# Two passes over the weights become three, in a single-core decoder step (SSD scan, gMLP gating, expert retrieval)

## The chip, the cores and the metric

The kernel runs on one NeuronCore of a Trainium2 chip. The metric is the device time of one execution in microseconds, lower is better; the state before is given as the median of three executions. All data are float32.

## The reference, cut to what matters

One decoder layer is applied to 512 prompt tokens (one sequence) and to 8 samples of one token each, with the same weights (D = 2048).

```python
proj = x @ w_in                                   # z, xbc, dt, u, v, gates
xbc  = silu(causal_conv(xbc))                     # 4 taps
y, new_ssm = ssd_scan(xh, dt, A, B, C, state)     # chunks of 128 tokens, state carried on
y_a  = rms_per_group(y_with_skip * silu(z)) * w   # 8 groups
v    = layer_norm(gelu(v));  y_b = gelu(u) * (tril(W_s) @ v + b)     # per chunk of 128
mix  = (sigmoid(ga) * (y_a @ w_a) + sigmoid(gb) * (y_b @ w_b)) @ w_out
h    = layer_norm(alpha * x + mix)
# PEER: 8 heads pick 16 of 16384 experts each, by product keys
q = h @ w_q;  expert, gate = product_key_top16(q)
out  = sum_k gate_k * gelu(h . peer_u[expert_k]) * peer_v[expert_k]
y    = layer_norm(alpha * h + out)
```

Outputs are y of both groups, the last conv rows, the final SSD states of prompt and samples, and the normalised v of the last chunk. Every token gathers 128 rows of `peer_u` and 128 rows of `peer_v` of 8 KB each.

## The kernel before, in words

**Tiles.** All weights are laid out as 224 tiles of 128 output channels by 2048 inputs (1 MB). `gemm` (line 400, its matmul on L409) multiplies one tile by the activations of a pass: 16 matmuls of 128 x 128 weights with n columns, n being the tokens of the pass; a float32 matmul shows as two MATMUL instructions, each with a LDWEIGHTS, so a tile has 32 of each. The tiles come through a ring of three buffers (`load_weight`, L396) from SP's queue; tile p is loaded once tile p - 3 has been used.

**Passes.** Activations of all tokens don't fit into SBUF beside the rest, so the layer runs in two passes, each over all 224 tiles: pass A with 256 prompt tokens and the 8 samples (264 columns), pass B with the other 256 tokens. A pass has three stages, with a barrier after each: `ssd` (80 tiles), `sgu` (32 tiles) and `back` (112 tiles: 32 gates, 16 of w_b, 32 of w_a, 16 of w_out, 16 of w_q).

**Scan stage.** For each of 8 groups, TensorE projects B, C, four x tiles and four z tiles; ScalarE copies each to `raw` and makes the first tap, VectorE adds three (L1019), ScalarE applies silu (L927). Then for each chunk of 128 tokens `chunk_a` transposes and forms C B (L842 to L844), ScalarE makes the decays, VectorE weighs them (`weigh`, L1054 to L1056), and `chunk_b` multiplies (L857, L859, L860). The gated result is normalised (`rms` L865, `finish`) and stored to DRAM. A chunk's decay rows come by a DMA of 0.5 MB.

**The samples' scan** (pass A only) is GpSimd's: per group eight units of 4 samples x 128 states (128 x 512 elements): load the state, multiply by the decay (L1193), form x dt B (L1195), add (L1197), store (L1198), multiply by C (L1201); VectorE sums (L1037). B and C rows of a group go through DRAM (L1183, L1185), so that all partitions get them. The samples' eight columns are part of `xg` and `yg` and are normalised with the prompt's.

**SGU and back.** `sgu` projects V, normalises it (`ln_*`), projects U, mixes per chunk. `back` projects the gates, multiplies with both branches, adds and normalises to h, and in its last 16 tiles scores q against the keys and selects experts on VectorE (`Selection`, top 16 of each side, then of the 256 sums). The samples' selection is finished in pass B (`smp`).

**Experts.** There is one slot for each of the 512 tokens' j-th expert rows in a block (4 blocks x 128) and 8 slots for the samples: 520 in all. A slot gathers one `peer_u` row and one `peer_v` row for each of 128 tokens (two indirect DMAs of 1 MB, L250, from GpSimd's queue), and VectorE multiplies and sums with h (L306, 2.3 us) and adds the weighted v rows (L327, 2.35 us). Experts of a block can be fetched once that block's choice is done. So pass A has no slots; `plan` writes 260 slots by hand into the order of pass B (14 in each of the 8 scan groups, 20 + 20 in `sgu`, 32, 16, 32 and 16 with the tiles of `back`, 3 in the norm, 9 in the choice), and `tail` does the other 260 after the passes, with eight buffers each for u and v where the passes have four.

Of the kernel before, what the change touches and what calls it, by code (L numbers as in the profile page):

```python
# [25 lines left out]
P = 128  # L26
# [45 lines left out]
RING = 3  # L72
PASSES = 2
CP = CH // PASSES
NP = CP * P
# [8 lines left out]
SLOTS = CP * P  # L84
LAG = 6

# [14 lines left out]
class Pass:  # L101


    def __init__(self, i):
        self.i, self.smp = i, i == 0
        self.n = NP + (NS if self.smp else 0)
        self.first = NP * i
        self.col = 0 if i == 0 else NP + NS
        self.pos = N_TILES * i
        self.grp = N_GROUPS * i  # L110
        self.rows = [P] * CP + ([NS] if self.smp else [])
        self.nb = len(self.rows)

# [93 lines left out]

class Experts:
# [44 lines left out]
    def u_row(self, pool, s):  # L253

        if s < self.total:
            b, j = self.items[s]
            if not self.is_sample(s) and j % TOPK == 0:
                pool.wait_ge(self.k.head_done, PH * (b // CP) + j // TOPK + 1)
# [11 lines left out]
    def rows(self, pool, s, ahead, u_from=0):  # L270


        if s + ahead >= u_from:
            self.u_row(pool, s + ahead)
        if s - self.lag + ahead >= u_from:
            self.v_row(pool, s - self.lag + ahead)
# [71 lines left out]
class Kernel:  # L348
# [41 lines left out]
    def load_weight(self, sp, p):  # L390

        if p >= PASSES * N_TILES:
            return
        if p >= RING:
            sp.wait_ge(self.w_used, p - RING + 1)
        sp.dma_start(self.w_ring[:, p % RING, :],  # L396
                     self.a["w_tiles"][ORDER[p % N_TILES]]).then_inc(self.w_in[p % RING], 16)

    def gemm(self, pe, p, grp, x, n, start=True, stop=True, x_ready=None):
# [5 lines left out]
        pe.wait_ge(self.w_in[p % RING], 16 * (p // RING + 1))  # L405
        for k in range(KB):
            if x_ready:
                pe.wait_ge(*x_ready(k))
            last = pe.matmul(o, self.w_ring[:, p % RING, k * P:(k + 1) * P], x[:, k, :],  # L409
# [12 lines left out]
    def plan(self):  # L422
# [4 lines left out]
        def put(key, n):  # L427
            nonlocal s
            at[key] = range(s, s + int(n))
            s = at[key].stop  # L430

        for g in range(G):
            for c in range(9):
                put(("ssd", g, c), 1 + (c in (1, 3, 5, 7, 8)))
        for n in range(FT):
            put(("v", n), 1 + (n % 4 == 1))
        for n in range(FT):
            put(("u", n), 1 + (n % 4 == 1))
        for c in range(2 * FT):
            put(("gate", c), 1)  # L440
        for n in range(FT):
            put(("wb", n), 1)
        for n in range(FT):
            put(("wa", n), 2)
        for n in range(FT):
            put(("out", n), 1)
        put(("ln", 0), 2)
        put(("ln", 1), 1)
        for n in range(FT):
            put(("q", n), n >= 7)  # L450
# [3 lines left out]
    def steps(self, ps, *key):  # L454

        return self.at[key] if ps.i == 1 else ()

    def span(self, *names):

        every = [s for key, r in self.at.items() if key[0] in names for s in r]  # L460
        return range(min(every), max(every) + 1)


    def build(self):
# [12 lines left out]
        passes = [Pass(i) for i in range(PASSES)]  # L477
        self.pass_a = passes[0]
        with self.root:
# [20 lines left out]
            with ExitStack() as gemm:  # L500
                gs = lambda name, shape: gemm.enter_context(nc.sbuf_tensor(name, shape, F32))
                self.w_ring = gs("w_ring", [P, RING, WCOLS])
# [5 lines left out]
                with ExitStack() as st:  # L508
                    n = passes[0].n
                    cut = self.region(flat(rows_a))  # L510
                    xs, yb, m_acts = cut(KB, n), cut(KB, n), cut(KB * n)
                    spare = st.enter_context(nc.sbuf_tensor("spare", [P, KB * n], F32))[:]
                    self.tables(xs)
                    self.clear_sems()
                    self.one_pass(passes[0], xs, spare, yb, m_acts, None)
# [1397 lines left out]
```

## Time and profile before

| | us |
|---|---|
| median of 3 executions | 5422.86 (5422.43 to 5433.51) |
| profiled execution | 5416.87 |
| its span, first to last instruction | 5414.9 |
| TensorE busy | 3608.6 (67%) |
| VectorE busy | 3422.2 (63%) |
| GpSimd busy | 2398.3 (44%) |
| ScalarE busy | 702.4 (13%) |
| moved by DMA | 1672.07 MB, 309 GB/s on average |

Pass A lies between 56 and 1910 us of the span, pass B between 1910 and 4067, the tail after that. The busy shares are averages over these three parts, which have different limits; they must be read stage by stage. Matmuls are pipelined and their ends are modelled, so the distance between the starts of two groups of instructions tells more of TensorE's pace than the mean duration of one.

### The profile page before, as it was taken

The numbers are of one execution on the slowest core, as the hardware profiler recorded it, in microseconds if no ns is written. First come the engines' busy times: TensorE is split into PE (matmuls) and PEld (weight loads), VectorE is DVE, ScalarE is ACT, GpSimd is POOL, SyncE is SP. The second block draws the span as 40 slices with busy tenths as digits, with TensorE's granted clock in tenths as the row PEclk, the third lists the DMA queues.
The fourth block names the chain that finished last, engine by engine and source line by source line (L and its number), as shares of the span: only waits on it lengthen the run. The fifth ranks groups of instructions, "written<-read, shape, count | busy, mean of one in ns | idle before, by whom it ended". The sixth has DMA issues, their size and how long they took to land. (4 is left out here: it accounts for less than half of the span.)

```text
span 5414.9 us, 43573 instructions
## 1 busy us (share of the span) xinstructions
PE 3608.6 (67%) x16560; PEld 3028.1 (56%) x16560; DVE 3422.2 (63%) x4133; ACT 702.4 (13%) x1501; POOL 2398.3 (44%) x1504
## 2 busy tenths in 40 slices
PE   7999979999999968888778697897940000230000
PEld 5787768888887757667667586786740000000000
DVE  3455531000001859989867665565798999789999
ACT  2232321000000123333311010000100000000000
POOL 3575730000000025545543432443318888778885
PEclk8999989999999989999889898998975555565555
DMA  5565643344444379999989899999749999999998
GB/s 175 192 217 196 210 156 132 133 148 164 164 156 140 126 301 405 421 420 410 421 356 377 351 421 384 389 421 412 307 155 398 420 422 422 422 380 422 422 422 363
DMA packets 275097, 1672.07 MB, mean 309 GB/s; under 512 B 37041, under 2 KB 66225, under 8 KB 81969
## 3 DMA queue, kind: packets, MB, share of 16 engines
q0 software_dynamic: 161920, 1133.78, 51.2%
q1 hardware_dynamic: 112968, 535.51, 26.4%
q8 instruction: 131, 2.15, 0.2%
q14 instruction: 78, 0.63, 0.0%
HBM read 1633.31 MB, written 35.79 MB: 308 GB/s over the span
## 5 line engine op out<-in xcount | busy, mean ns | idle before, releaser
L250 POOL DMA_INDIRECT rows_a<-in_peer_u,expert x384 | 819.0, 2133 | 2182.4 <-POOLq L369 1149.2
L409 PE MATMUL psum<-rows_a,w_ring 128*128 128x264 f32 x7168 | 1625.5, 388 | 24.1 <-PEq L369 18.9
L409 PEld LDWEIGHTS psum<-rows_a,w_ring 128*128 128x128 f32 x7168 | 1367.2, 191 | 265.5 <-issue 30.5
L409 PE MATMUL psum<-x_acts,w_ring 128*128 128x256 f32 x5632 | 1257.4, 384 | 131.0 <-PEq L369 57.5
L409 PEld LDWEIGHTS psum<-x_acts,w_ring 128*128 128x128 f32 x5632 | 1084.0, 193 | 287.9 <-issue 83.4
L306 DVE SCALAR_TENSOR_TENSOR rows_a<-rows_a,h_tokens 128x2048 f32<-128x2048 f32 x384 | 878.7, 2289 | 106.1 <-DMA rows_a<-in_peer_u,expert 75.9
L250 POOL DMA_INDIRECT rows_a<-in_peer_v,expert x384 | 593.3, 1545 | 333.2 <-DVE h_tokens L327 165.1
L327 DVE SCALAR_TENSOR_TENSOR h_tokens<-rows_a,coef,h_tokens 128x2048 f32<-128x2048 f32 x256 | 602.6, 2354 | 79.4 <-issue 73.5
L1744 PE MATMUL psum<-acc,selector 8*128 8x512 f32 x64 | 57.5, 1075 | 683.8 <-DVE rows_a L306 479.0
L1744 PEld LDWEIGHTS psum<-acc,selector 8*128 8x128 f32 x64 | 19.9, 325 | 720.0 <-DVE rows_a L306 485.3
L1019 DVE SCALAR_TENSOR_TENSOR conv_acc<-raw,g_par,conv_acc 128x256 f32<-128x256 f32 x288 | 175.5, 609 | 283.8 <-ACT conv_acc L913 277.0
L327 DVE SCALAR_TENSOR_TENSOR acc<-rows_a,coef,acc 128x2048 f32<-128x2048 f32 x128 | 300.9, 2350 | 32.8 <-issue 30.2
L327 DVE SCALAR_TENSOR_TENSOR h_tokens<-rows_b,coef,h_tokens 128x2048 f32<-128x2048 f32 x128 | 300.9, 2351 | 20.2 <-issue 16.2
L306 DVE SCALAR_TENSOR_TENSOR rows_b<-rows_b,h_tokens 128x2048 f32<-128x2048 f32 x128 | 293.0, 2290 | 27.3 <-DMA rows_b<-in_peer_u,expert 22.6
L286 ACT ACTIVATE gelu<-dots 128x4 f32<-128x4 f32 x130 | 26.7, 205 | 2140.3 <-DVE rows_a L306 1517.1
L250 POOL DMA_INDIRECT rows_b<-in_peer_u,expert x128 | 265.5, 2074 | 81.5 <-issue 37.2
L250 POOL DMA_INDIRECT rows_b<-in_peer_v,expert x128 | 252.9, 1976 | 51.1 <-issue 37.4
L409 PE MATMUL psum<-branch_b,w_ring 128*128 128x256 f32 x1024 | 229.7, 385 | 43.6 <-DMA w_ring<-in_w_tiles 29.1
L409 PEld LDWEIGHTS psum<-branch_b,w_ring 128*128 128x128 f32 x1024 | 197.8, 194 | 72.6 <-issue 43.1
L1622 DVE TENSOR_TENSOR rows_a<-rows_a,psum 128x264 f32<-128x264 f32 x16 | 6.9, 429 | 338.3 <-PE psum L409 338.3
L1631 DVE TENSOR_TENSOR branch_part<-spare,psum 128x264 f32<-128x264 f32 x16 | 6.9, 429 | 214.2 <-PE psum L409 214.2
L409 PE MATMUL psum<-merged,w_ring 128*128 128x256 f32 x512 | 115.2, 384 | 1.8 <-DVE merged L1634 1.8
(368 smaller groups left out, 3024.8 us busy)
## 6 DMA issues: line engine op xcount, KB each, us to landing
w_ring<-in_w_tiles SPq DMA_DIRECT2D x448, 1024.0 KB, 6.3
smp_state<-in_state_ssm POOLq DMA_DIRECT2D x64, 256.0 KB, 5.7
out_ssm_sample<-smp_state POOLq DMA_DIRECT2D x64, 256.0 KB, 3.1
rows_a<-acum_rows_dram SPq DMA_DIRECT2D x16, 512.0 KB, 7.4
BC_bcast<-smp_bc_dram POOLq DMA_DIRECT2D x8, 1024.0 KB, 5.0
branch_b<-acum_rows_dram SPq DMA_DIRECT2D x16, 512.0 KB, 12.4
rows_a<-in_peer_u,expert POOLq DMA_INDIRECT x384, 20.6
rows_a<-in_peer_v,expert POOLq DMA_INDIRECT x384, 21.1
```

Of the source, the lines that this page charges most:

```text
L250: return pool.indirect_dma_start(out=dst, out_offset=None, in_=table, in_offset=bass.IndirectOffsetOnAxis(ap=self.index(s), axis=0))
L286: act.activation(self.ge[:, c], self.dots[:, c], ACT.Gelu).then_inc(self.gelu_done, 1)
L306: dve.scalar_tensor_tensor(out=u, in0=u, scalar=1.0, in1=h, op0=ALU.mult, op1=ALU.mult, accum_out=self.dots[:, s % 8:s % 8 + 1]).then_inc( ...
L327: dve.scalar_tensor_tensor(out=acc, in0=self.vrow[self.slot[s]], scalar=self.coef[:, s % 8:s % 8 + 1], in1=acc, op0=ALU.mult, op1=ALU.add) ...
L409: last = pe.matmul(o, self.w_ring[:, p % RING, k * P:(k + 1) * P], x[:, k, :], start=start and k == 0, stop=stop and k == KB - 1)
L1019: ins = dve.scalar_tensor_tensor(out=ac, in0=r[:, k:k + NP], scalar=w[:, k:k + 1], in1=ac, op0=ALU.mult, op1=ALU.add)
L1622: self.out_of_bank(dve.tensor_tensor(merged[:, m, :], merged[:, m, :], self.bank[(G_WB + m) % 2][:, 0:n], ALU.mult), G_WB + m)
L1631: self.out_of_bank(dve.tensor_tensor(part[:, m % 2, :], ga[:, m, :], self.bank[(G_WA + m) % 2][:, 0:n], ALU.mult), G_WA + m)
L1744: last = pe.matmul(self.bank[c], sel[:, b, :], h_smp[:, 512 * c:512 * (c + 1)], start=True, stop=True)
```

## The change

There are three passes: 128 tokens with the samples (136 columns), 128 tokens, and 256 tokens; each goes over all 224 tiles, so 672 tiles are loaded instead of 448. The ring has four buffers in the first two passes and three in the last. Of the 260 slots that the passes take, 80 are now in the second pass (4 in each scan group, 4 with V, 7 with U, 8 with the gates, 4 and 8 with w_b and w_a, 7 with w_out, 2 in the norm, 8 in the choice) and 180 in the third (10 in each scan group, then 12, 14, 22, 12, 22, 10, 2, 6). The tail keeps its 260.

The samples' scan is written anew (`Samples`): four units a group of 8 samples x 128 states; GpSimd updates the states of group g once all of the group's silu are done, and VectorE multiplies by C and sums them during group g + 1 (`sums`, after conv 2, 3, 4 and 5). SP, no longer GpSimd, stores the B and C rows. The last group's units run in the SGU stage, and the gate, skip and norm of all samples are done there once for all groups (`gated`, a matmul, a square root, `scaled`), and stored for `back`. ScalarE makes silu of the samples' columns in instructions of their own. In a pass with one chunk, `chunk_b` stands after the last z tile, and the next group's first conv after the gating.

```diff
-RING = 3
-PASSES = 2
-CP = CH // PASSES
-NP = CP * P
+PASS_CHUNKS = ((0, 1), (1, 1), (2, 2))
+PASSES = len(PASS_CHUNKS)
+RINGS = (4, 4, 3)
...
+STEPS_B = (4, 4, 7, 8, 4, 8, 7, 2, 8)
+STEPS_C = (10, 12, 14, 22, 12, 22, 10, 2, 6)
...
+class Samples:
+    BUFS = 3
...
+    def load(self, pool, v):
+        r = v - self.first
+        if r >= self.BUFS:
+            pool.wait_ge(self.state_out[r % self.BUFS], 16 * (r // self.BUFS))
+            pool.wait_ge(self.summed, r - self.BUFS + 1)
+        pool.dma_start(self.state[:, r % self.BUFS], self.source[v]).then_inc(self.state_in[r % self.BUFS], 16)
+
+    def load_bc(self, pool, g):
+        if GT * g > self.first:
+            pool.wait_ge(self.summed, GT * g - self.first)
+        pool.dma_start(self.bc[:].rearrange("p m b n -> p (m b n)"),
...
+    def unit(self, pool, o, v, stop):
+        g, t, r = v // GT, v % GT, v - self.first
+        s, decay, dt = self.state[:, r % self.BUFS], self.k.dt_smp[:, g, 1, t, :], self.k.dt_smp[:, g, 0, t, :]
+        if v + 2 < stop:
+            self.load(pool, v + 2)
+        o(pool.tensor_tensor(dt, dt, self.x[:, g, t, :], ALU.mult))
+        pool.wait_ge(self.state_in[r % self.BUFS], 16 * (r // self.BUFS + 1))
+        pool.tensor_tensor(s, s, bc(decay, NST), ALU.mult)
+        pool.wait_ge(self.bc_in, 16 * (r // GT + 1))
+        o(pool.tensor_tensor(self.xb[:], self.bc[:, 0], bc(dt, NST), ALU.mult))
+        o(pool.tensor_tensor(s, s, self.xb[:], ALU.add))
+        pool.sem_inc(self.ready, 1)
+        pool.dma_start(self.target[v], s).then_inc(self.state_out[r % self.BUFS], 16)
...
+    def sums(self, dve, o, v):
+        r = v - self.first
+        dve.wait_ge(self.ready, r + 1)
+        dve.wait_ge(self.bc_in, 16 * (r // GT + 1))
+        o(dve.tensor_tensor(self.prod[:], self.state[:, r % self.BUFS], self.bc[:, 1], ALU.mult))
+        dve.tensor_reduce(self.y[:, v // GT, v % GT, :], self.prod[:], AX_X, ALU.add).then_inc(self.summed, 1)
+        dve.wait_ge(self.summed, r + 1)
...
     # load_weight
-        if p >= RING:
-            sp.wait_ge(self.w_used, p - RING + 1)
...
+        while self.loaded < PASSES * N_TILES and self.loaded - RINGS[self.loaded // N_TILES] <= p:
...
     # build
-                    self.one_pass(passes[0], xs, spare, yb, m_acts, None)
...
+                    self.first_pass(passes[0], rows_a)
+                    self.later_pass(passes[1], ex)
+                self.later_pass(passes[2], ex)
...
     # ssd, SP
+                        if t == 5 and ps.smp:
+                            sp.wait_ge(bc_ready, g + 1)
+                            sp.dma_start(self.bc_dram[g].rearrange("m b n -> b m n"), bcs[:]).then_inc(bc_out, 16)
...
     # ssd, TensorE
-                    chunk_b(g, 0)
-                    chunk_a(g, 1)
+                    if nc_ > 1:
+                        chunk_b(g, 0)
+                        chunk_a(g, 1)
                     project(g, CT + 3)
+                    if nc_ == 1:
+                        chunk_b(g, 0)
...
     # ssd, VectorE
                     conv(g, 2)
+                    sum_smp(g - 1, 0)
...
                     conv(g, 5)
+                    sum_smp(g - 1, 3)
...
     # ssd, GpSimd
+                        pool.wait_ge(conv_done, CT * g + CT)
+                        pool.dma_start(out["conv_sample"][g], scv[:, g % 2, 1:4]).then_inc(conv_out[g % 2], 16)
+                        if g > 0:
+                            load_conv(g + 1)
+                        if g < G - 1:
+                            pool.wait_ge(bc_out, 16 * (g + 1))
+                            smp.load_bc(pool, g)
+                            pool.wait_ge(silu_done, CT * g + CT)
+                            for t in range(GT):
+                                smp.unit(pool, o, GT * g + t, GT * (G - 1))
...
     # sgu, SP
+                    if smp and m == FT + 14:
+                        sp.wait_ge(smp_done, 1)
+                        sp.dma_start(self.ys.rearrange("n p t -> p n t")[:, 0:G * GT, ps.col + np_:ps.col + n],
+                                     smp.y[:].rearrange("p g t b -> p (g t) b")).then_inc(smp_out, 16)
...
     # sgu, VectorE
+                    if smp and 4 <= m < 4 + GT:
+                        smp.sums(dve, o, GT * (G - 1) + m - 4)
+                    if smp and m == 8:
+                        smp.gated(o, dve, self.gp[:, :, GP_D:GP_D + GT]).then_inc(sq_ready, 1)
```

## Rows read from the trace of the kernel before

**Rows 1.** The page, the span in 40 equal slices

```profile
PEclk8999989999999989999889898998975555565555
DMA  5565643344444379999989899999749999999998
GB/s 175 192 217 196 210 156 132 133 148 164 164 156 140 126 301 405 421 420 410 421 356 377 351 421 384 389 421 412 307 155 398 420 422 422 422 380 422 422 422 363
```

**Rows 2.** Busy time by stage; after ACT and POOL: granted clock, DMA share, GB/s

```profile
core 0: us, PE busy (x) PEld busy (x) DVE busy (x) ACT busy (x) POOL busy (x), PEclk, DMA share, GB/s
56.00:780.00 724.00, 662.00 (x3169) 550.37 (x3170) 371.03 (x586) 222.82 (x505) 433.56 (x448) 0.95 0.57 197
780.00:1045.00 265.00, 258.09 (x1184) 219.99 (x1183) 33.58 (x61) 26.45 (x56) 0.00 (x0) 0.98 0.39 135
1045.00:1764.00 719.00, 710.68 (x3176) 604.78 (x3177) 44.42 (x89) 20.70 (x41) 0.00 (x0) 1.00 0.43 151
1764.00:1910.00 146.00, 125.45 (x618) 104.19 (x616) 123.02 (x502) 17.63 (x52) 0.00 (x0) 0.94 0.33 117
1910.00:1938.00 28.00, 0.25 (x1) 0.25 (x2) 0.45 (x3) 0.19 (x1) 7.65 (x8) 0.50 0.92 358
1938.00:2762.00 824.00, 667.03 (x3280) 572.34 (x3280) 703.96 (x758) 283.97 (x566) 418.87 (x218) 0.90 0.97 401
2762.00:3085.00 323.00, 254.88 (x1184) 222.22 (x1184) 215.68 (x189) 28.15 (x66) 134.69 (x80) 0.90 0.92 374
3085.00:3311.00 226.00, 225.48 (x1030) 197.52 (x1031) 152.44 (x138) 36.38 (x58) 78.11 (x62) 0.99 0.98 402
3311.00:3872.00 561.00, 476.23 (x2144) 414.31 (x2143) 350.38 (x309) 10.15 (x25) 225.19 (x134) 0.92 0.97 398
3872.00:4067.00 195.00, 118.06 (x576) 103.96 (x574) 167.74 (x537) 21.71 (x42) 26.08 (x16) 0.81 0.44 157
4067.00:5415.00 1348.00, 87.79 (x128) 25.84 (x128) 1242.54 (x894) 27.64 (x80) 1072.58 (x526) 0.51 0.99 411
```

**Rows 3.** TensorE in order of time, 3885 to 3897 us: start, us, instructions

```profile
3886.89 0.61 PE L1517 MATMUL psum<-branch_b 128*128 128x128 f32 x4
3887.34 0.60 PE L1527 MATMUL psum<-ident,x_acts 128*128 128x128 f32 x4
3887.77 7.07 PE L409 MATMUL psum<-x_acts,w_ring 128*128 128x256 f32 x32
3894.68 0.61 PE L1517 MATMUL psum<-branch_b 128*128 128x128 f32 x4
```

**Rows 4.** DMA queues, from 2000 to 2700 us, then from 780 to 1047 us

```profile
q0 software_dynamic: 27751, 202.13, 69.3%
q1 hardware_dynamic: 17669, 87.87, 30.7%
...
q1 hardware_dynamic: 7104, 35.74, 38.3%
```

**Rows 5.** Groups of instructions on GpSimd, from 100 to 760 us

```profile
L1197 POOL TENSOR_TENSOR smp_state<-smp_state,smp_x_dt 128x512 f32<-128x512 f32 x63 | 92.9, 1475 | 4.9
L1195 POOL TENSOR_TENSOR smp_x_dt<-BC_bcast,dt_smp 128x512 f32<-128x512 f32 x63 | 68.1, 1081 | 22.6 <-DMA BC_bcast<-smp_bc_dram 22.6
L1193 POOL TENSOR_TENSOR smp_state<-smp_state,dt_smp 128x512 f32<-128x512 f32 x63 | 66.8, 1060 | 3.1
L1198 POOL DMA_DIRECT2D out_ssm_sample<-smp_state x63 | 50.5, 802 | 19.3 <-POOL smp_state L1197 19.3
```

**Rows 6.** Groups on VectorE: a product in pass A's scan, the same in pass B's

```profile
L1055 DVE TENSOR_TENSOR spare<-spare,cb_masked 128x1024 f32<-128x1024 f32 x16 | 32.0, 2003 | 0.5
...
L1055 DVE TENSOR_TENSOR h_tokens<-h_tokens,cb_masked 128x1024 f32<-128x1024 f32 x14 | 17.2, 1226 | 0.5
```

**Rows 7.** TensorE's waits: who for whom, us in total, times, longest

```profile
PE psum L857 <- DVE h_tokens L1056: 70.9, 15, 12.5
PE psum L409 <- DMA x_acts<-in_xT: 48.3, 1, 48.3
```

**Rows 8.** The page's costliest groups: pass A's matmuls and their weight loads

```profile
L409 PE MATMUL psum<-rows_a,w_ring 128*128 128x264 f32 x7168 | 1625.5, 388 | 24.1 <-PEq L369 18.9
L409 PEld LDWEIGHTS psum<-rows_a,w_ring 128*128 128x128 f32 x7168 | 1367.2, 191 | 265.5 <-issue 30.5
```

More of the change, by code:

```diff
@@ L454, in steps, with span @@
     def steps(self, ps, *key):
[L456 to L461, printed above, removed]
+        return self.at.get((ps.i,) + key, ())
+    def span(self, ps, *names):
+        return [s for key, r in self.at.items() if key[0] == ps.i and key[1] in names for s in r]
     def build(self):
@@ L477, in build @@
         passes = [Pass(i) for i in range(PASSES)]
+        ring = [p % RINGS[p // N_TILES] for p in range(PASSES * N_TILES)]
+        last, self.w_slot, self.w_turn, self.w_held, self.loaded = {}, ring, [], [], 0
+        for p, slot in enumerate(ring):
+            self.w_held.append(last.get(slot, -1))
+            self.w_turn.append(ring[:p].count(slot))
+            last[slot] = p
         self.pass_a = passes[0]
@@ L1138, in _ @@
                     expert(g, 8)
+                    if nc_ == 1 and g < G - 1:
+                        conv(g + 1, 0)
                 finish(G - 1)
@@ L1147, in _ @@
                         ex.v_row(pool, s)
-                    for s in self.span("ssd"):
-                        ex.rows(pool, s, 4, 4)
+                if ex:
+                    for s in self.span(ps, "ssd"):
+                        ex.rows(pool, s)
                 if ps.smp:
@@ L1293, in _ @@
                 def _(pool):
-                    for s in self.span("v", "u"):
-                        ex.rows(pool, s, 4, 4)
+                    for s in self.span(ps, "v", "u"):
+                        ex.rows(pool, s)
+            if smp:
+                @block.gpsimd
+                def _(pool):
+                    o = Chain(pool, pord)
+                    first, stop = GT * (G - 1), GT * G
+                    smp.load(pool, first)
+                    smp.load(pool, first + 1)
+                    smp.load_bc(pool, G - 1)
+                    for v in range(first, stop):
+                        smp.unit(pool, o, v, stop)
+                    smp.stored(pool)
             @block.tensor
@@ L1327, in _ @@
                     last.then_inc(mixed, 1)
+                    if smp and m == 9:
+                        pe.wait_ge(sq_ready, 1)
+                        for t in range(GT):
+                            last = pe.matmul(self.bank[2][:, 0:G * NS], self.onesG[:], smp.x[:, :, t, :],
+                                             start=(t == 0), stop=(t == GT - 1))
+                        last.then_inc(rms_done, 1)
             @block.scalar
@@ L1601, in _ @@
                 for c in range(2 * FT):
[L1602 removed]
+                    if pick and c == 2:
                         for s in range(2):
```

470 lines of the change are left out of this document (236 added, 234 removed).

## The prediction, made before the changed kernel was seen

> **What bounds the kernel now.** I read the page's 40 slices first: the transfers run at 126 to 217 GB/s through the first 14 slices, mostly at 350 to 422 GB/s from slice 16 on, and TensorE is granted its high level (2.4 GHz) almost throughout the passes [rows 1]. Then I cut the span at the stage edges [rows 2]. Pass A (samples and 256 tokens) ends at 1910 us. TensorE is busy in 1757 of its 1854 us, and the DMA engines are half idle (shares 0.57, 0.39, 0.43, 0.33). Pass B (256 tokens, with 260 of the 520 expert slots in its order) takes 2157 us, and there the DMA share is 0.92 to 0.98 in all stages but the last. The tail takes 1348 us at 411 GB/s. So A is TensorE's, B and the tail are the transfers'. The last stage of a pass, the expert choice, is VectorE's: 123 of 146 us busy.
>
> **Unit prices.** A float32 matmul is two instructions here, so a 1 MB weight tile is 32. With 256 columns, 32 of them take 3894.68 - 3887.77 = 6.91 us, or 216 ns each; with 128 columns and a fresh weight load before each, eight take 3887.77 - 3886.89 = 0.88 us, or 110 ns [rows 3]. A tile therefore costs 6.9 us at 256 columns, 3.5 at 128, and, interpolated, 3.7 at 136; in pass A (264) it is 7.1. On the DMA engines, in B's scan, the queue of the gathers moved 202.13 MB in 69.3% of 700 us (417 GB/s) and that of the weights 87.87 MB in 30.7% (409 GB/s): 2.56 us a tile (1.049 MB) and 5.03 us an expert slot (two gathers of 1.049 MB). In A's SGU stage the weights' queue gives 35.74 MB in 38.3% of 267 us, 349 GB/s or 3.0 us a tile [rows 4].
>
> **The change part by part.** It adds 224 tiles (235 MB) and, at 128 or 136 columns, saves none of TensorE's column time: the two narrow passes' 3.7 + 3.5 us replace 7.1. What it can win is 80 slots leaving the last pass for the middle one, where TensorE leaves DMA time over.
>
> *First pass, scan.* Today 724/8 = 90.5 us a group. TensorE would need 10 x 3.7 + some 5 for one chunk = 42. POOL: four units of double size instead of eight, the product with C moved to VectorE; 2 x (1.06 + 1.08 + 1.48) = 7.2 us of arithmetic and two issues, between 0.80 (as now) and 1.6 each, I take 1.05, and 0.5 of the rest, 9.8 a unit, 39 a group, 44 with the waits for B and C rows [rows 5]. The DMA share says 0.57 x 724/8 = 51.6 us a group, all of it still there but one of two decay rows (0.5 MB, 1.4 us): 50 [rows 2]. I take 52, transfers first. Ends: 42 (packets give way) and 90.5 - 10 x 3.4 = 57 (nothing else shrinks). With start and edge 8 x 52 + 12 = 428. VectorE gets four products (1024 elements) and four sums a group. A 1024-element product takes 1.23 us alone and 2.00 while POOL computes [rows 6], the sum some 1.2: 4 x 3.2 = 13 us, in room left by half-width work; if that cover is gone, 13 us a group, 104 in all. The waits added: VectorE waits for POOL's unit before conv 3, 4, 5 of the next group, and conv, silu and TensorE's chunk stand behind it; POOL is due first by a third of a unit. POOL waits for all four sums before the next B/C load; SP now issues the B/C store, waiting for a ScalarE copy that is some 8 us old by then, ahead of weights for which it has a ring of four. I cost these at nothing beyond the 52.
>
> *First pass, rest.* SGU: 265 - 32 x 3.4 = 156; group 8's units (about 45 us of POOL) lie beside 59 us of V tiles, the gated norm beside U tiles; the 32-byte rows of the samples' store (4,096 of them) land during the last tiles, 0 to 10 us, taken 0. Gates to output: 96 tiles, 719 - 96 x 3.4 = 393. Choice: 146 us; per-block instructions halve, chained waits don't: ends 73 and 123, taken 99, as most instructions here are of the per-block kind. With the 56 before the scan: 56 + 428 + 156 + 393 + 99 = **1132**, for 1910.
>
> *Middle pass* (80 slots: 32 in the scan, 11 in SGU, 8 + 4 + 8 + 7 + 2 = 29 from the gates to the norm, 8 in the choice). Its bound is transfers. Checked on today's B: scan 8 x (25.6 + 14 x 5.03 + 3.3 of rows) = 794 for 824; SGU 82 + 40 x 5.03 + 5 = 288 for 323; gates to norm 246 + 99 x 5.03 + 10 = 754 for 787: it loses about 30 a stage to edges and late tiles. So: start 25 (eight gathers and x; today 28, and TensorE waited 48.3 for x [rows 7]), scan 8 x (25.6 + 20.1 + 3.3) + 25 = 417 (TensorE needs 41 of each 49), SGU 82 + 55 + 5 + 30 = 172, gates to norm 246 + 29 x 5.03 + 10 + 33 = 435, choice 94 + 8 x 4.7 of VectorE = 132. Sum **1181**; lower end without the losses, -88; upper end with 3.0 us a tile, +99.
>
> *Last pass* (180 slots: 80, 26, 68 and 6 in the same stages). Per scan group: transfers 25.6 + 10 x 5.03 + 3.3 = 79, TensorE 69 + 13 = 82; today TensorE waited 70.9 us on VectorE's weighing in 15 chunks [rows 7], of which I keep about half: 88 (ends 82 and today's 103). 28 + 8 x 88 + 19 = 751. SGU 32 x 6.9 + the 38 that A spends beside its tiles + 17 edge = 276 (transfers 218). Gates to norm 96 x 6.9 + 35 (A's own excess) + 20 of late branch rows = 717 (transfers 598). Choice: A 146 without slots, B 195 with 9, so 146 + 33 = 179. Sum **1923**, for 2157: 80 slots x 5.03 = 402 us of transfers go, only 234 come back, for TensorE is late next.
>
> The tail stays, 1348. **Sum** 1132 + 1181 + 1923 + 1348 = 5584, for a span of 5415: +169. The profiled execution took 2 us more than its span, the median of the runs shown 6 more again: 5592, said as **5590**.
>
> **The weight-load rule.** Eight narrow pairs ran at 110 ns [rows 3], so loads hid; but the row of pass A gives a load a mean of 191 ns, against 227 for its matmul's busy time [rows 8], and no burst longer than eight is on record. The Trainium skill ("TensorE: Matmul & The Clock Gate", section "Back-to-back issue gap") says that in a stream of load and matmul pairs at 128 columns the load shows: some 81 ns where an isolated matmul takes about 56. By that ratio the tile would be 5.1 us instead of 3.5, an estimate from the page, and the sum near 6010.
>
> **Rivals.**
> 1. *The engines overlap cleanly* (faster). Narrow passes leave every engine slack, so no wait is passed on: A's scan at TensorE's 42 (-80), the middle pass at its transfers alone (-88), the last scan at 82 (-48): 5584 - 216 = 5368, given as 5375. It decides once 169 of these 216 are won. For it: TensorE is 99% busy in today's gates [rows 2]. Against: today's B, just as slack on TensorE, loses 30 us a stage.
> 2. *Weight loads bind in the narrow passes.* Upper bound, 191 ns an instruction, 6.1 us a tile: A's groups 52 to 68 (+128), its SGU +77, its gates to output +230; the middle scan 49 to 70 (+168), SGU +53, gates to norm 96 x 6.1 = 586 + 30 for 435 (+181): 5592 + 837, about 6430. At a pitch between the two, 135 ns and 4.3 us a tile, it is 0.6 x 128 tiles in the first pass and little elsewhere, about 5680.
> 3. *The clock falls in the middle pass.* Where TensorE waits for transfers the granted clock falls: 0.90 in B's scan and SGU, 0.81 in its choice, 0.50 while it waits for x, against 1.00 in A's gates [rows 2]. At 0.65, TensorE's 41 us a group become 63 for 49 (+112), 96 tiles at 5.4 give 518 + 30 for 435 (+113), SGU some +40: about 5855; at 0.80 its 51 us barely bind, +20. The same page of the Trainium skill (section "HAM oscillation — how this bites in real kernels") speaks against narrow passes: a kernel with 128 rows falls back to half clock at each wait for data, and it says to keep TensorE fed or the operand wide. Here the trace agrees as to sign only.
> 4. *No change.* Rival 1 wins most but not all of its sum, near 5423.
>
> The change cannot simply fail to act: the slots are written into the order of every engine.
>
> **How the numbers follow.** Forecast 0.67, rival 1 0.14, rival 2 0.06, rival 3 0.08, rival 4 0.05. A measurement of this kernel tells 0.2%, 11 us, from no change; only rival 1 is faster, 0.14 and 0.01 of the forecast's own lower tail. The forecast's bounds (A -105/+75, middle -88/+99, last -60/+120) seldom meet at one end: 5470 to 5710. Down to 5400 it takes in rival 4 and rival 1's upper half, up to 5750 the mild forms of 2 and 3; some 0.15 stays outside.
>
> **What would show it.** After: bytes 1672 + 235 = 1907 MB; 32 matmul instructions of 136 columns in 3.7 us in the first pass's gates; first pass's end near 1132, groups 52 us apart with a DMA share near 1; middle pass at about 420 GB/s and 1181 us, TensorE at a granted clock near 0.9; last pass 1923 us with TensorE over 90% busy in gates and DMA share below 0.9; tail 1348. Wrong if narrow tiles take over 4 us, if A's groups keep TensorE's 42 us, or if the last pass takes under 1850.

## The result, and the profile after

The changed kernel takes 5597.8 us (median of 4, 5589.9 to 5612.0) where the kernel before takes 5422.7: 1.033 times as long, 95% interval 1.0314 to 1.0341. The forecast was 5590, slower. The profiled execution took 5589.9 us, its span 5588.1.

The page's slices, after:

```profile
PEclk8888999989989999799998989999995555565555
DMA  6777778779998999699998789889847999999998
GB/s 238 251 257 256 265 269 295 253 292 414 415 360 344 378 391 369 241 384 396 381 402 339 293 345 379 340 333 370 314 166 296 419 422 422 422 381 422 422 422 362
```

Against [rows 1] the first eight slices are fuller of transfers, and the stretch of 340 to 415 GB/s begins at slice 10 and not 16: that is the middle pass. In the last pass a single slice still passes 400. Moved in all were 1916.42 MB (forecast 1907).

Busy time by stage, after (columns as in [rows 2]); the lines are the four stages of the first pass, start and four stages of the middle one, the four of the last, and the tail:

```profile
61.00:558.00 497.00, 347.07 (x2840) 338.10 (x2840) 256.48 (x442) 151.89 (x472) 242.67 (x191) 0.85 0.74 263
558.00:714.00 156.00, 137.60 (x1144) 136.20 (x1144) 37.12 (x76) 22.85 (x59) 33.35 (x25) 0.95 0.76 262
714.00:1099.00 385.00, 374.40 (x3174) 373.16 (x3175) 29.80 (x89) 14.77 (x40) 0.00 (x0) 0.99 0.78 275
1099.00:1168.00 69.00, 69.00 (x568) 63.55 (x567) 56.97 (x238) 13.96 (x44) 0.00 (x0) 1.00 0.64 229
1168.00:1198.00 30.00, 1.06 (x6) 0.64 (x6) 16.52 (x67) 1.02 (x5) 7.64 (x8) 0.57 0.46 164
1198.00:1592.00 394.00, 340.00 (x2952) 327.99 (x2952) 257.80 (x394) 166.77 (x422) 102.22 (x58) 0.95 1.00 410
1592.00:1763.00 171.00, 133.61 (x1137) 131.58 (x1137) 71.17 (x95) 20.14 (x59) 43.32 (x22) 0.90 0.87 345
1763.00:2182.00 419.00, 367.89 (x3138) 362.58 (x3138) 156.71 (x199) 24.85 (x55) 100.38 (x55) 0.95 0.96 383
2182.00:2325.00 143.00, 68.94 (x560) 67.43 (x560) 121.80 (x354) 15.93 (x37) 34.86 (x20) 0.77 0.71 268
2333.00:3049.00 716.00, 648.37 (x3281) 558.31 (x3281) 573.04 (x661) 268.15 (x547) 310.18 (x160) 0.95 0.92 376
3049.00:3336.00 287.00, 253.39 (x1185) 222.21 (x1186) 150.46 (x143) 27.82 (x63) 97.45 (x52) 0.93 0.80 319
3336.00:4061.00 725.00, 695.22 (x3166) 609.13 (x3166) 347.57 (x308) 36.56 (x67) 249.81 (x132) 0.98 0.86 341
4061.00:4239.00 178.00, 117.48 (x580) 103.97 (x578) 154.73 (x527) 19.05 (x40) 15.19 (x12) 0.83 0.41 148
4239.00:5588.00 1349.00, 87.05 (x128) 25.73 (x128) 1243.52 (x894) 27.56 (x80) 1074.32 (x526) 0.51 0.99 411
```

One stage stands out. The first scan takes 497 us, 62 a group, and nobody is full in it: TensorE 347 us, transfers 0.74, GpSimd 243. In the next passes the picture is the forecast's: the middle scan at a DMA share of 1.00, the last pass's gates with TensorE at 695 of 725 us.

TensorE in order of time in the first pass's output stage, as [rows 3] showed it at 256 columns:

```profile
1043.31 3.87 PE L504 MATMUL psum<-rows_a,w_ring 128*128 128x136 f32 x32
1047.01 0.39 PE L1288 MATMUL psum<-rows_a,onesD 128*128 128x136 f32 x2
1047.24 3.87 PE L504 MATMUL psum<-rows_a,w_more 128*128 128x136 f32 x32
```

A tile of 136 columns takes 1047.01 - 1043.31 = 3.70 us, 116 ns an instruction, as interpolated; no weight load shows.

Now the first scan. Waits from 61 to 558 us: who for whom, us in total, times, longest:

```profile
ACT smp_x L1034 <- DVE conv_acc L1138: 167.9, 22, 16.7
PE psum L943 <- ACT rows_a L1035: 138.0, 7, 21.1
DVE smp_prods L283 <- POOLq L269: 136.7, 16, 13.3
POOL rows_a L247 <- DMA out_ssm_sample<-rows_a: 103.3, 17, 8.8
```

Together these lines are one chain: TensorE waits for ScalarE's silu, ScalarE for the convolution, VectorE for a state unit of GpSimd ahead of that convolution, and GpSimd for a store. The timeline, 320 to 343 us, shows one turn of it:

```profile
320.68 0.94 POOL L270 DMA_DIRECT2D out_ssm_sample<-rows_a  x1 [0.61 <-POOL rows_a L268]
321.86 1.22 DVE L284 TENSOR_REDUCE smp_y<-smp_prods 128x8 f32<-128x1024 f32 x1
...
330.40 0.88 POOL L247 DMA_DIRECT2D rows_a<-in_state_ssm  x1 [8.78 <-DMA out_ssm_sample<-rows_a]
...
331.60 1.89 POOL L265 TENSOR_TENSOR rows_a<-rows_a,dt_smp 128x1024 f32<-128x1024 f32 x1
333.45 1.89 POOL L267 TENSOR_TENSOR smp_x_b<-smp_bc,dt_smp 128x1024 f32<-128x1024 f32 x1
335.42 2.34 POOL L268 TENSOR_TENSOR rows_a<-rows_a,smp_x_b 128x1024 f32<-128x1024 f32 x1
337.90 1.22 DVE L283 TENSOR_TENSOR smp_prods<-rows_a,smp_bc 128x1024 f32<-128x1024 f32 x1 [13.32 <-POOLq L269]
338.37 0.94 POOL L270 DMA_DIRECT2D out_ssm_sample<-rows_a  x1 [0.61 <-POOL rows_a L268]
339.16 1.22 DVE L284 TENSOR_REDUCE smp_y<-smp_prods 128x8 f32<-128x1024 f32 x1
340.41 1.13 DVE L1130 SCALAR_TENSOR_TENSOR conv_acc<-raw,g_par,conv_acc 128x128 f32<-128x128 f32 x3
...
342.13 0.39 ACT L1035 ACTIVATE rows_a<-conv_acc,g_par 128x128 f32<-128x128 f32 x1
...
342.56 1.12 PE L943 MATMUL psum<-ident,rows_a 128*128 128x128 f32 x4 [20.68 <-ACT rows_a L1035]
```

The first thing in `unit` v is the load of unit v+2. With three buffers it takes the place of unit v-1, whose store was issued the instruction before, so GpSimd stands 8.78 us until that store has landed, and needs 7.5 us more (330.40 to 337.90) until the unit is ready. VectorE has been standing 13.32 us at the product, with the last convolution behind it, and TensorE 20.68.

The same load also waits for VectorE's sum of unit v-1. In this turn that sum was done at 321.86 + 1.22 = 323.08 us, so the last 7.3 us before 330.40 are the store's alone. Over the scan the trace puts 103.3 us (17 waits) down to stores and 23.4 (2 waits) to sums.

### The profile page after: what moved, and what is told of

Its sections match the earlier page's. It is cut to its first block and busy times, and to the rows that moved or that the text cites. A ratio compares the mean times of both kernels' runs of the same rounds, so it can differ in the third digit from the quotient of the medians.

```text
span 5588.1 us, 59888 instructions
## 1 busy us (share of the span) xinstructions
PE 3668.2 (66%) x23928; PEld 3335.1 (60%) x23928; DVE 3490.7 (62%) x4551; ACT 818.0 (15%) x1999; POOL 2312.9 (41%) x1272
## 2 busy tenths in 40 slices
DMA packets 325902, 1916.42 MB, mean 343 GB/s; under 512 B 44320, under 2 KB 85856, under 8 KB 103648
## 5 line engine op out<-in xcount | busy, mean ns | idle before, releaser
L504 PE MATMUL psum<-x_acts,w_ring 128*128 128x256 f32 (+1 forms) x9984 | 1787.0, 341 | 264.9 <-DMA w_ring<-in_w_tiles 96.2
L343 POOL DMA_INDIRECT rows_a<-in_peer_u,expert x384 | 911.9, 2375 | 2334.5 <-DVE rows_a L399 1711.1
L504 PEld LDWEIGHTS psum<-x_acts,w_ring 128*128 128x128 f32 x9984 | 1602.9, 196 | 431.6 <-issue 203.4
L504 PE MATMUL psum<-rows_a,w_ring 128*128 128x136 f32 x5376 | 655.1, 283 | 23.7 <-PEq L462 17.9
L504 PEld LDWEIGHTS psum<-rows_a,w_ring 128*128 128x128 f32 x5376 | 645.7, 194 | 30.9 <-issue 29.8
L1130 DVE SCALAR_TENSOR_TENSOR conv_acc<-raw,g_par,conv_acc 128x128 f32<-128x128 f32 (+1 forms) x432 | 212.3, 491 | 247.5 <-ACT conv_acc L1018 236.4
L504 PE MATMUL psum<-branch_b,w_ring 128*128 128x256 f32 (+1 forms) x1664 | 303.4, 344 | 23.8 <-DMA branch_b<-branch_acts 21.5
L504 PE MATMUL psum<-rows_a,w_more 128*128 128x136 f32 x1792 | 221.4, 283 | 0.0
L504 PEld LDWEIGHTS psum<-rows_a,w_more 128*128 128x128 f32 x1792 | 216.4, 194 | 0.4 <-issue 0.4
L504 PE MATMUL psum<-merged,w_ring 128*128 128x256 f32 (+1 forms) x896 | 161.8, 340 | 3.7 <-DMA w_ring<-in_w_tiles 3.7
```

The source lines that it names most:

```text
L343: return pool.indirect_dma_start(out=dst, out_offset=None, in_=table, in_offset=bass.IndirectOffsetOnAxis(ap=self.index(s), axis=0))
L504: last = pe.matmul(o, w[:, k * P:(k + 1) * P], x[:, k, :], start=start and k == 0, stop=stop and k == KB - 1)
L1130: ins = dve.scalar_tensor_tensor(out=ac, in0=r[:, k:k + np_], scalar=w[:, k:k + 1], in1=ac, op0=ALU.mult, op1=ALU.add)
```

## The experiments

**The fourth buffer.** My theory: the wait for the store makes the 62 us. Rivals: VectorE's order, or the transfers.

```diff
-    BUFS = 3
+    BUFS = 4
```

> One more buffer for the samples' states, so that the load of unit v+2 takes the place of unit v-2, whose store was issued two units before, and not of unit v-1. Theory (store before reload): in the changed kernel's first scan GpSimd waits 103 us in 17 waits for the store that it has just issued, VectorE then waits 137 us in 16 waits for GpSimd's units, and the convolutions behind them keep TensorE waiting about 20 us a group, so that a group takes 62 us where 52 was forecast. With the wait gone the first scan falls from 497 us to about 425, the waits of GpSimd for the store to under 20 us, and the whole to about 5525 us (5510 to 5545). Rival 1 (VectorE's order alone: sums stand ahead of convolutions, whatever the buffers): less than 15 us are gained, 5585 to 5600. Rival 2 (transfers: the states' loads, stores and the weights share the queues): the wait goes over to the loads of the states or of the weights, 5585 to 5610.

Measured: 5520.9 us (1.018, 1.0164 to 1.0198), 77 less and in the theory's range. The first scan of this kernel, and then its waits:

```profile
61.00:480.00 419.00, 342.46 (x2818) 334.05 (x2817) 281.00 (x433) 149.35 (x469) 249.27 (x188) 0.91 0.88 309
```

```profile
POOL rows_a L247 <- DVE smp_y L284: 68.4, 12, 10.5
PE psum L943 <- ACT rows_a L1035: 75.7, 7, 11.5
```

The scan is 419 us and the store's wait is gone. GpSimd now waits for VectorE's sums, and TensorE still 10.8 us a group.

**The load behind the store.** The same wait shortened without memory.

```diff
-        if v + 2 < stop:
-            self.load(pool, v + 2)
         o(pool.tensor_tensor(dt, dt, self.x[:, g, t, :], ALU.mult))
...
         pool.dma_start(self.target[v], s).then_inc(self.state_out[r % self.BUFS], 16)
         self.last = r
+        if v + 2 < stop:
+            self.load(pool, v + 2)
```

> Three buffers as in the changed kernel, but the load of unit v+2 is issued at the end of unit v, behind its store, and not at its start. The store that it waits for is then one unit (about 10 us of GpSimd's own work) older, and the load has one unit instead of two to land. Theory (store before reload): most of the wait goes, the first scan takes 425 to 450 us and the whole 5525 to 5555 us. If only the number of buffers counts, or VectorE's order, or the transfers: 5585 to 5610. If the loads land later than a unit: a wait for the state's load appears, and the scan stays over 470 us.

Measured: 5528.2 us (1.020, 1.018 to 1.0214), 70 less, and the waits for the state's load come to 4.4 us. So the number of buffers is not what counts, but what a load has to wait for. Both cures loosen the wait for the sum too: a unit can then be worked on before the sum of the one before it is done. No run loosened one of the two waits by itself; that the store is the larger one here is read from the trace alone (103.3 against 23.4 us).

**The sums later in VectorE's order**, with three buffers and with four:

```diff
                     conv(g, 2)
-                    sum_smp(g - 1, 0)
...
                     conv(g, 4)
-                    sum_smp(g - 1, 2)
+                    sum_smp(g - 1, 0)
...
                     conv(g, 5)
-                    sum_smp(g - 1, 3)
+                    sum_smp(g - 1, 1)
                     expert(g, 4)
                     spread_chunk(g, 0)
+                    sum_smp(g - 1, 2)
...
                     weigh(g, 0)
+                    sum_smp(g - 1, 3)
```

(The sum behind conv 3 goes too.)

> Three buffers as in the changed kernel, but the four sums of a group stand later in VectorE's order: the first two behind the convolutions 4 and 5, the third behind the spread, the fourth behind the weighing, so that two of them hold back no convolution. Theory (store before reload): GpSimd's cycle of about 15.5 us a unit stays, and the loads that also wait for the sum of the unit before come no sooner; the first scan stays at 480 to 530 us, the whole at 5580 to 5630. Rival 1 (VectorE's order alone): the convolutions run ahead, TensorE's wait of 20 us a group goes, the first scan takes about 430 us and the whole 5530.

Measured with three: 5601.8 us (1.034, 1.0321 to 1.0359), no gain. In its scan, to 480 us:

```profile
DVE smp_prods L283 <- POOLq L269: 164.6, 17, 14.1
PE psum L958 <- DVE spare L1163: 108.2, 6, 21.4
POOL rows_a L247 <- DMA out_ssm_sample<-rows_a: 100.1, 16, 9.5
```

The convolutions run free, and waits of up to 21 us, as before, turn up at the weighed products (L958), since GpSimd's cycle is as it was. VectorE's order alone was not the cause.

> Four buffers for the samples' states and the four sums later in VectorE's order, as in the run with three buffers that had them later. With the store's wait gone, GpSimd waits 68 us in the first scan for VectorE's sums and TensorE about 10 us a group for the convolutions and transposes. Theory (VectorE's order is what is left): the convolutions run ahead and the first scan falls from 419 us to 380 to 400, the whole to 5490 to 5510. Rival 1 (GpSimd's own work of about 44 us a group is what is left, with the load of the broadcast rows that waits for the last sum): later sums hold GpSimd up more, 5515 to 5560. Rival 2 (no effect): 5515 to 5527.

Measured with four: 5487.5 us (1.013, 1.0115 to 1.0152), another 33 less, just below the theory's range; TensorE's wait for silu falls from 75.7 to 37.0 us. With GpSimd ahead, the order counts. Its first scan:

```profile
61.00:450.00 389.00, 342.43 (x2824) 333.80 (x2822) 287.92 (x435) 151.77 (x470) 262.82 (x189) 0.94 0.91 334
```

**No units in the first scan:** the floor. With four buffers, this kernel leaves out the samples' state of groups 0 to 6, so it does not compute all the outputs.

```diff
-                    if ps.smp and g >= 0:
-                        smp.sums(dve, o, GT * g + t)
+                    pass
...
                         if g < G - 1:
                             pool.wait_ge(bc_out, 16 * (g + 1))
-                            smp.load_bc(pool, g)
-                            pool.wait_ge(silu_done, CT * g + CT)
-                            for t in range(GT):
-                                smp.unit(pool, o, GT * g + t, GT * (G - 1))
```

(The first two state loads and the last wait for the stores go too.)

> Four buffers, and the samples' state units of groups 0 to 6 (GpSimd's products and sums, their loads and stores, the broadcast rows, VectorE's products and sums) are left out of the first scan; the samples' convolutions stay, and the last group's units. It is the floor of the first scan. Theory (the units still set it, through VectorE's order): the scan falls from 419 us to about 350, set by ten tiles of 3.7 us and the chunk's steps, and the whole to 5450 (5435 to 5470). Rival 1 (the chain of convolution, transpose, weighing and output of one narrow chunk sets it, with or without the samples): 400 to 420 us, the whole 5500 to 5522. Rival 2 (the weights' transfers set it): it falls by what the states' 59 MB of loads and stores took, about 140 us at 410 GB/s, as far as TensorE's tiles let it: below 350.

Measured: 5431.0 us (1.002, 1.0012 to 1.0031), a little below the theory's range. The first scan is 327 us, 41 a group; the number is that of rival 2, but not its mechanism, for the DMA share is 0.81. Nor are the states' transfers 59 MB, as the expectation has it: the whole program moves 1916.42 MB with them and 1879.70 without, 37 MB. The view of the scan:

```profile
61.00:388.00 327.00, 326.07 (x2819) 319.06 (x2817) 131.73 (x377) 149.29 (x469) 7.51 (x14) 1.00 0.81 284
```

TensorE is busy throughout at its high level. A narrow group can run at TensorE's pace (the forecast's lower end, 42); the samples' units cost 170 us as written, 92 with four buffers, 62 with the order changed too. The clock is a small part of it: TensorE's own busy time is 347 us at a granted 0.85 as written and 326 at 1.00 here, 21 of the 170 us. VectorE's own slowness beside GpSimd may be another part; how much of these us it makes was not separated. The convolution's step without the units, and then with them and four buffers:

```profile
L1131 DVE SCALAR_TENSOR_TENSOR conv_acc<-raw,g_par,conv_acc 128x128 f32<-128x128 f32 x144 | 50.7, 352 | 105.9 <-ACT conv_acc L1018 102.2
```

```profile
L1130 DVE SCALAR_TENSOR_TENSOR conv_acc<-raw,g_par,conv_acc 128x128 f32<-128x128 f32 x144 | 112.8, 783 | 52.9 <-ACT conv_acc L1018 48.9
```

The same 144 instructions take 352 ns alone and 783 beside a GpSimd that is busy 249 of 419 us. The Trainium skill ("SBUF — State Buffer", section "Who interferes with whom") says that a VectorE instruction with two SBUF inputs contends with a GpSimd instruction that reads SBUF, because its second input comes through a read interface that both share. These rows agree with it: the convolution's step reads two tiles of SBUF.

**Where the slots go.** None, 40 or 112 of the 260 in the middle pass, for 80 (the run with 40 has four buffers and later sums, that with 112 four buffers). The edit for none:

```diff
-STEPS_B = (4, 4, 7, 8, 4, 8, 7, 2, 8)
-STEPS_C = (10, 12, 14, 22, 12, 22, 10, 2, 6)
+STEPS_B = (0, 0, 0, 0, 0, 0, 0, 0, 0)
+STEPS_C = (14, 20, 20, 32, 16, 32, 16, 3, 9)
```

> No expert slot in the middle pass; the last pass carries all 260 again, spread as the kernel before spread them. Theory (prices of the prediction): the middle pass, which is set by transfers at a share of 1.00 in its scan, becomes bound by TensorE at 3.7 us a tile and takes about 1015 us instead of 1157; the last pass, where a slot costs 3 us more, takes about 2157 instead of 1914; the whole comes to about 5700 us (5660 to 5740). Rival 1 (the transfers are the bound in both passes and the slots only change place): within 20 us of 5598. Rival 2 (the slots are free in the middle pass, TensorE sets it): the last pass's 240 us come back in full, 5820 to 5860.

> Four buffers, and 112 expert slots in the middle pass where the changed kernel has 80; 148 in the last. The run with none in the middle showed 195 us in the middle for 80 slots (2.44 each) and 224 in the last (2.8 each). Theory (in the middle pass each further slot costs its whole transfer, 5.03 us, since the queues are at a share of 1.00 there, and the last pass gives back 2.8 to 3.0): 32 slots cost 161 and give back 93, so 5521 becomes about 5589 (5570 to 5610). Rival (every slot costs the mean of 2.44): 5505 to 5520, and still more slots would be better.

> Three passes, four buffers, sums later (5488 us with 80 slots in the middle), and 40 slots in the middle. Shown so far: from 0 to 80 slots the middle pass takes 195 us more, from 80 to 112 another 143 (4.5 each); the last pass gives back 224 us for the first 80 and almost nothing for the next 32. Theory (both convex: a slot costs nothing much until the transfers are full, and its whole transfer after; the last pass gives back its transfer until TensorE sets it): the middle is shorter by 110 to 150 us, the last longer by 80 to 112, the whole 5450 (5430 to 5475). Rival (both straight): 5488 minus 98 plus 112, 5495 to 5510.

Measured: none 5620.8 us (1.036, 1.0345 to 1.038), below the theory's range; 112, 5650.8 (1.0425, 1.0407 to 1.0442), above it; 40, 5437.4 (1.003, 1.0021 to 1.0044), within it. To keep the first scan out, I take the middle pass from its load of x to the last pass's, and the last one from there to its second load of x, at the merge (the few slots behind it are not in these numbers). Busy time of these stretches; first no slots in the middle:

```profile
1190.00:2133.00 943.00, 879.12 (x7786) 868.34 (x7786) 259.36 (x786) 191.10 (x527) 7.64 (x8) 0.97 0.78 277
```

Then 40, both passes:

```profile
1079.00:2113.00 1034.00, 895.56 (x7786) 882.53 (x7786) 426.66 (x910) 210.27 (x550) 140.50 (x82) 0.93 0.86 328
2113.00:3738.00 1625.00, 1463.97 (x7028) 1269.29 (x7029) 1148.02 (x1141) 338.63 (x685) 726.38 (x390) 0.96 0.95 390
```

The changed kernel itself, 80, both passes:

```profile
1187.00:2325.00 1138.00, 910.68 (x7786) 889.82 (x7786) 607.49 (x1040) 227.69 (x571) 288.43 (x162) 0.92 0.93 372
2325.00:3904.00 1579.00, 1459.70 (x7029) 1271.49 (x7030) 987.80 (x1027) 326.12 (x667) 611.80 (x320) 0.96 0.88 356
```

And 112, the middle pass:

```profile
1114.00:2395.00 1281.00, 935.54 (x7786) 909.29 (x7786) 751.94 (x1144) 233.43 (x583) 403.44 (x226) 0.89 0.94 382
```

| slots in the middle | middle pass, us | last pass to the merge, us |
|---|---|---|
| 0 | 943 | 1766 |
| 40 | 1034 | 1625 |
| 80 | 1138 | 1579 |
| 112 | 1281 | 1569 |

(With four buffers, 80 slots take 1141 and 1586.) Both columns bend, as the theory for 40 had it; of its two terms the middle pass gave 104 us (110 to 150 expected) and the last pass took 46 (80 to 112 expected). In the middle pass a slot costs 2.3 us, 2.6, then 4.5 as the queues fill. The last pass gives back 3.5 us a slot for the first 40, 1.2 for the next, and 0.3 for the last 32, for at 80 its DMA share is only 0.88 and TensorE is busy for 1460 of 1579 us. This is what the expectation for 112 missed: it had the last pass give back 93 us for these 32 slots. The 80 of the change are past the best: 80 in place of 40 cost some 50 us (5487.5 against 5437.4). My expectation for none, 5700, was 80 too high: it priced these slots at 1.8 us in the middle (measured 195 / 80 = 2.4) and 3.0 in the last pass in place of 2.8 (224 us, since the tail's first matmul came 33 us later after a last pass begun 192 us earlier).

**Two passes, with the samples' scan of the change** and its loads at the end of a unit:

```diff
-PASS_CHUNKS = ((0, 1), (1, 1), (2, 2))
+PASS_CHUNKS = ((0, 2), (2, 2))
...
-RINGS = (4, 4, 3)
+RINGS = (3, 3)
...
+STEPS_B = (14, 20, 20, 32, 16, 32, 16, 3, 9)
```

> The changed kernel put back to two passes of 264 and 256 columns with a ring of three and all 260 slots in the second pass, but with the new scan of the samples (units of GpSimd a group behind, their norm in the next stage), its loads issued at the end of a unit. It tells what the samples' scan is worth without the third pass. Theory (the third pass costs, the samples' scan gains): the first scan, 785 us in the kernel before with TensorE busy for 723 of them, loses part of the 62 us in which TensorE stood idle and comes to about 740; the whole to 5375 us (5345 to 5400). Rival 1 (the samples' scan moves nothing, since TensorE sets the first scan of two passes): 5405 to 5435. Rival 2 (GpSimd's units and VectorE's product contend with the convolutions of twice the width): over 5440.

> Two passes as in the run of two passes, but with the loads of the states at the start of a unit, three buffers, as in the changed kernel: GpSimd waits for the store that it has just issued. A group of two chunks lasts about 84 us there, GpSimd's four units 44 us and the four waits for stores some 24 to 32. Theory (the store's wait costs only where a group is shorter than GpSimd's units with their waits): it is hidden, 5355 to 5375 us. Rival (VectorE's sums in order hold up the convolutions at any group length): the wait shows here too, 5390 to 5430.

> Two passes with the new scan of the samples and its loads at the end of a unit, as in the run of two passes, and the four sums of a group later in VectorE's order. TensorE is busy for 662 of 683 us in the first scan of that run, so at most some 20 us are left there. Theory (TensorE sets the first scan of two passes): 5345 to 5362 us. Rival (later sums hold up VectorE's outputs behind the weighing, with two chunks in a group): 5365 to 5400.

Measured: loads at the end 5359.4 us (0.989, 0.9874 to 0.9907), **faster than the kernel before**; loads at the start, as the change has them, 5420.2 (0.9997, 0.9987 to 1.0006); later sums on top of loads at the end 5379.5 (0.993, 0.9917 to 0.9944). Busy time from 57 to 740 us, loads at the end and then at the start; the second kernel gets less far in these 683 us (3039 of TensorE's instructions for 3237):

```profile
57.00:740.00 683.00, 661.93 (x3237) 553.27 (x3236) 383.37 (x545) 232.71 (x571) 266.63 (x200) 0.98 0.60 207
```

```profile
57.00:740.00 683.00, 635.43 (x3039) 532.13 (x3039) 327.98 (x520) 219.70 (x549) 246.84 (x191) 0.96 0.57 195
```

I had expected the store's wait to be hidden in groups of 84 us; instead the place of the loads costs all of the 61 us that the new scan is worth. The waits of the run with loads at the start, first scan:

```profile
POOL rows_a L246 <- DVE smp_y L283: 251.9, 7, 47.4
DVE smp_prods L282 <- POOLq L268: 110.8, 12, 11.3
POOL rows_a L246 <- DMA out_ssm_sample<-rows_a: 70.4, 12, 9.2
```

GpSimd stands 36 us a group for a sum, and then VectorE for GpSimd. Unit 1 begins with the load of unit 3, which waits for the sum of unit 0, and VectorE takes that one a group later; so GpSimd is one unit ahead and no more, and units 1 to 3, each with the wait for its store, fall into the short stretch of convs 3 to 5. So a longer group does not hide the waits; this account is read from the code and the trace. With the load at the end GpSimd still waits 230.7 us for sums, in 13 waits, but it is a unit further ahead: VectorE's wait for it is gone, and TensorE's for silu falls from 47.6 to 7.0 us. How much of the 61 us is the store and how much that further unit was not separated.

The later sums, 33 us won in the narrow pass, lose 20 here, as the rival had it: ScalarE's wait for VectorE's state (L1106) goes from 48.5 to 73.6 us and TensorE's for its result (L961) from 5.1 to 18.3. It looks as if with two chunks a group the stretch behind the weighing is the one that is short; that was not tested further.

**The ring of three in the narrow passes**, with four buffers (5520.9):

```diff
-RINGS = (4, 4, 3)
+RINGS = (3, 3, 3)
```

> Four buffers for the samples' states (5521 us), and the ring of weight tiles back to three buffers in the two narrow passes as well. A narrow tile takes TensorE 3.7 us, its transfer 2.56 at the full rate, and in the changed kernel TensorE waited for w_ring 102 us in 49 waits, most in the middle pass, whose queues are at a share of 1.00. Theory (a full queue is not made faster by a deeper ring; the depth only covers short lapses): 5520 to 5560 us, with the loss in the middle pass. Rival 1 (the fourth buffer is what lets a narrow pass keep TensorE fed: three tiles of 3.7 us are 11 us, about the 8 to 11 us from issue to landing of a loaded row of x): over 5600, and the first pass's tiles come over 4 us apart. Rival 2 (no effect): 5510 to 5530.

Measured: 5582.1 us (1.029, 1.0276 to 1.031), 61 more, between theory and first rival. Of that, 14 us are lost in the first pass and 61 in the middle one in the profiled execution (which was 13 above its median). Middle pass with a ring of three, then of four:

```profile
1124.00:2326.00 1202.00, 949.12 (x7786) 926.18 (x7786) 607.15 (x1040) 228.12 (x572) 290.67 (x162) 0.90 0.90 353
```

```profile
1110.00:2251.00 1141.00, 917.85 (x7786) 897.72 (x7786) 607.84 (x1040) 228.00 (x572) 289.00 (x162) 0.91 0.92 371
```

The theory that a full queue is not made faster by a deeper ring fails because the queue isn't full in the mean (0.92 with four tiles, 0.90 with three). The loss isn't in one place: the first gate tile starts 610 us after the pass's load of x instead of 580, and from there to the first tile of the choice it is 451 us instead of 420. TensorE's waits for the ring's tiles come to 106.0 us in the run with three and 71.9 with four.

## Why the prediction was right, and where it was not

The total was right to 0.1%, and partly by luck: one step was 69 us short (74 with the 5 us by which the scan began later), and the others together some 70 too long.

- **First pass, scan: the step that failed.** Forecast 428 us (52 a group), ending at 484; measured to 558. What failed is the sentence "the waits added ... I cost these at nothing beyond the 52". It said that GpSimd is due first by a third of a unit; in fact the load at the head of `unit` waits for the store just issued, a wait that I had not read out of `load` at all, and it passes down the chain to TensorE. Shown by the fourth buffer (419 us) and by the later load, each of which loosens that load's wait for the sum as well. The 104 us priced "if that cover is gone" are another mechanism, VectorE's own work with nothing to hide it; they would have given 428 + 104 = 532 us, for 497 measured. The 52 was right as a number, 52.4 with four buffers and the start and edge in it, and not for its reason: transfers do not bind there, for the share is 0.88, and 0.91 at 48.6 a group. The engines' time on transfers is 46 us a group (0.74 x 497 / 8), which I put at 50. GpSimd's unit is 0.88 + 1.89 + 1.89 + 2.34 + 0.94 = 7.9 us of work in the timeline, against 9.8 taken; VectorE's product took 1.22, not the 2.00 priced beside GpSimd: it waits for GpSimd instead of running beside it.
- **First pass, rest.** SGU 156 forecast, 156 measured; gates to output 393, 385; choice 99, 69: below even its lower end of 73, and TensorE's stage now (69 of 69 us busy, VectorE 57). The pass ended at 1168, for 1132.
- **Middle pass**: 1181, measured 2325 - 1168 = 1157. Start 25 and 30, scan 417 and 394 (share 1.00, 410 GB/s), SGU 172 and 171, gates to norm 435 and 419, choice 132 and 143. Right in its bound; the losses of 30 us a stage taken over from the kernel before were some 20 too many in the scan and 15 in the gates.
- **Last pass**: 1923, measured 4239 - 2325 = 1914: start and scan 751 and 724, SGU 276 and 287, gates to norm 717 and 725, choice 179 and 178. "80 slots x 5.03 go, only 234 come back, for TensorE is late next" holds: against 2157 it gives back 243; the run with none in the middle gives 224 for the same 80.
- The tail: 1348, measured 1349.
- **Rival 1**, clean overlap: its lower end for the first scan exists (41 us a group) but only without the units. **Rival 2**, weight loads: out, 3.70 us a tile; the Trainium skill's rule ("TensorE: Matmul & The Clock Gate", section "Back-to-back issue gap"), from which the prediction estimated 5.1, isn't what these float32 streams show. **Rival 3**, the clock: out, granted 0.95 in the middle scan, 0.90 in SGU, 0.95 in the gates; the same page's section "HAM oscillation — how this bites in real kernels" warned of half clock in narrow passes, which the busy stages of the middle pass don't show; the lowest clocks of the narrow passes are 0.77 in the middle pass's choice (TensorE busy 69 of 143 us) and 0.57 in its start (1 of 30). **Rival 4**, no change: out, 1.033.

So the change is two things of opposite sign and one mistake. The third pass, with its ring and its 80 slots, costs 169 us (5528.2 against 5359.4, same samples' scan); the best split tried, with the scan at its best, was still 0.3% above the kernel before, and 78 us above two passes with the load late. The new samples' scan gains 61 us (5420 to 5359), and its loads' place gives these 61 back, 70 in three passes.

## What to carry to other kernels

When a buffer is reused, read what its load waits for and when that was issued: a load at the head of a step that takes the place of the step just stored waits for that store to land (up to 9.5 us in these runs) and for whoever reads the buffer; put it at the end of the step, or add one buffer. A pass of fewer tokens repeats every weight tile, so it can pay only through work that finds free transfers there; stop adding such work where one more piece costs the pass what it gives back elsewhere (of 0, 40, 80 and 112 slots 40 was best, at a DMA share of 0.86). Take a change apart before dropping it: one part of this one, with its loads moved, is 1.1% faster than the kernel before.

## What was not expected of the hardware

- VectorE's convolution step took 352 ns without GpSimd's units, 639 with them as written (GpSimd busy 49% of the scan), 783 with four buffers (59%) and 730 with later sums as well (68%): 1.8 to 2.2 times as long, but not in step with GpSimd's share.
- GpSimd's operations of 1024 elements took 1.89, 1.89 and 2.34 us in the timeline, less than twice the 1.06, 1.08 and 1.48 of 512 [rows 5]; with later sums and four buffers their means were 2.10, 2.16 and 2.55.
- With tiles of 3.7 us on TensorE and 2.56 of transfer, a fourth tile in the ring was worth 61 us in all.
